# Three feature-major projections with token parts of 512, 512 and 32 moving columns in place of three of 352

## The reference, cut to what matters

```python
z = jnp.einsum('btd,de->bte', x, w_in)
mq, mk, mv, mo, mi, mf, aq, ak, av, iq, ik, iw = jnp.split(z, split_points, axis=-1)
mlstm = (heads(mq, M_HEADS), heads(mk, M_HEADS) * (M_HEAD_DIM ** -0.5), heads(mv, M_HEADS), mo, i_pre, log_f)
...
return h * jax.nn.sigmoid(o_pre), (C, n, m)      # o_pre is mo
```

## Time and profile before

| what | value |
|---|---|
| median of 3 runs | 1842.4 us (1838.47 to 1846.92) |
| the profiled execution's own time | 1841.46 us |
| its span, first to last instruction | 1839.6 us |
| mean granted TensorE clock | 0.954 of 2.4 GHz |
| PE busy | 1645.7 us (89% of the span) |
| DVE, ACT, POOL busy | 785.2, 471.7, 330.3 us |
| `fm` matmuls (L2090) | 864, in a stretch of 138.5 us |

### The profile page before, as it was taken

One profiled execution on the slowest core, in us unless ns is written; L12 is line 12 of the kernel. 1 busy time (PEld: TensorE's weight loads), 2 busy tenths in 40 slices (PEclk: granted clock), 3 DMA queues, 4 the chain that ended last, 5 costly groups with the idle time before them and its releaser, 6 DMA issues.

```text
span 1839.6 us, 28171 instructions
## 1 busy us (share of the span) xinstructions
PE 1645.7 (89%) x11020; PEld 1530.4 (83%) x11020; DVE 785.2 (43%) x1758; ACT 471.7 (26%) x942; POOL 330.3 (18%) x326
## 2 busy tenths in 40 slices
PE   7989999999987685887886899999999999999984
PEld 6855999999975564567886899999999999999983
DVE  2055999991224452254225532322322323313337
ACT  3264222121323342224114411111111111110013
POOL 3520452122200000100000322222221211212004
PEclk9979999999999898998997899999999999999996
DMA  5200211222243004113110321111111111111002
GB/s 161 70 7 26 65 51 48 90 89 94 71 126 130 13 24 162 46 46 128 44 45 1 92 69 47 47 42 31 51 41 47 46 47 47 46 46 46 1 23 95
DMA packets 122796, 110.36 MB, mean 60 GB/s; under 512 B 15778, under 2 KB 109606, under 8 KB 122674
## 3 DMA queue, kind: packets, MB, share of 16 engines
q1 hardware_dynamic: 122674, 108.61, 19.2%
HBM read 88.61 MB, written 19.95 MB: 59 GB/s over the span
## 4 chain that ended last, share of the span: by engine, by line
PE 41%; issue 14%; DVE 3%; ACT 0%; POOL 0%; DVEq 0%; ACTq 0%; POOLq 0%
PE bank L1577 27%; PE bank L1552 13%; DVE y_tm L1787 1%; DVE stats L1762 1%; PE bank L1008 0%; DVE y_acc L1560 0%; DVE hidden L1648 0%; ACT silu L1618 0%; POOL gate_up_split L1681 0%; DVE y_tm L1790 0%; PE bank L1719 0%; DVE hidden_split L1650 0%; PE bank L987 0%; PE bank L934 0%; POOL mv_by_sample L1137 0%
## 5 line engine op out<-in xcount | busy, mean ns | idle before, releaser
L1577 PE MATMUL bank<-x_split,gate_up_split 128*128 128x352 f32 x3168 | 517.0, 324 | 13.3 <-POOL gate_up_split L1681 6.6
L1577 PEld LDWEIGHTS bank<-x_split,gate_up_split 128*128 128x128 f32 x3168 | 510.5, 189 | 15.3 <-POOL gate_up_split L1681 6.9
L1552 PE MATMUL bank<-hidden_split,weight_split 128*128 128x352 f32 x1584 | 263.8, 326 | 15.7 <-DVE y_acc L1560 13.6
L2031 PE MATMUL bank<-w_split,xT_split 128*128 128x256 f32 (+1 forms) x2160 | 268.3, 284 | 7.4 <-POOL w_split L2237 7.4
L1552 PEld LDWEIGHTS bank<-hidden_split,weight_split 128*128 128x128 f32 x1584 | 257.7, 190 | 19.7 <-DVE y_acc L1560 17.4
L2031 PEld LDWEIGHTS bank<-w_split,xT_split 128*128 128x128 f32 (+1 forms) x2160 | 258.2, 181 | 10.5 <-issue 8.2
L1648 DVE TENSOR_TENSOR hidden<-silu,bank 128x352 f32<-128x352 f32 x66 | 34.4, 521 | 414.2 <-ACT silu L1618 414.0
L1681 POOL TENSOR_TENSOR gate_up_split<-gate_up,gate_up_split 128x2048 fp32r<-128x2048 f32 x22 | 101.6, 4618 | 593.6 <-ACT gate_up_split L1610 593.6
L1560 DVE TENSOR_TENSOR y_acc<-y_acc,bank 128x352 f32<-128x352 f32 x264 | 136.3, 520 | 119.1 <-PE bank L1552 119.1
L2326 DVE TENSOR_SCALAR_CACHE_REDUCE chosen<-scores,level 128x384 uint8<-128x384 f32 (+2 forms) x198 | 174.3, 942 | 1.2
L2090 PE MATMUL bank<-xT_split,w_split 128*128 128x352 f32 x864 | 138.5, 323 | 0.0
(11 more groups left out here) (254 smaller groups left out, 1581.7 us busy)
## 6 DMA issues: line engine op xcount, KB each, us to landing
w_unit<-in_w_in_dram SPq DMA_DIRECT2D x16, 1024.0 KB, 5.6
gate_up<-in_w_gate_dram SPq DMA_DIRECT2D x22, 512.0 KB, 4.0
gate_up<-in_w_up_dram SPq DMA_DIRECT2D x22, 512.0 KB, 5.2
down_weight<-in_w_down_dram SPq DMA_DIRECT2D x11, 1024.0 KB, 5.0
scratch_dram<-feature_stage SPq DMA_DIRECT2D x36, 176.0 KB, 1.8
scores<-in_x_prompt_dram SPq DMA_DIRECT2D x8, 512.0 KB, 5.8
out_dram<-stage SPq DMA_DIRECT2D x32, 128.0 KB, 1.7
out_weight<-in_w_out_dram SPq DMA_DIRECT2D x8, 512.0 KB, 4.4
```

The source lines that it names most:

```text
L1552: mm = pe.matmul(PS[6 + n % 2][:, 0:CH], wds[:, a, k, d * P:(d + 1) * P], hs[:, 2 * s + k, b, c * CH:(c + 1) * CH], start=(k == 0 and (a, ...
L1577: mm = pe.matmul(PS[2 * c + w][:, 0:CH], gs[:, u, a, w, k, :], xs[:, b, k, c * CH:(c + 1) * CH], start=(k == 0 and (a, b) == PARTS[0]), st ...
L2031: mm = pe.matmul(bank[0:rows(i), 0:HALF], xs1[:, a, k, tile_cols(i)], w[:, b, k, :], start=(k == 0 and (a, b) == PARTS[0]), stop=(k == KD ...
```

## The change

The 1,056 tokens of the `fm` jobs are cut at 512 and 1024. Parts 0 and 1 have 512 tokens, all of them prompt tokens, and part 2 has the 32 sample tokens. The number of jobs, matmuls and weight loads stays. The staging ring has 4 slots of 512 columns, no longer 6 of 352, because it lies in a fixed place. The index projection's `ikf` job (L2039) keeps its parts of 352.

```diff
-STG, FST, HALF = 8, 6, 256
+STG, FST, HALF = 8, 4, 256
+FM_COLS = [slice(0, 512), slice(512, 1024), slice(1024, T)]
...
-        fstage = put("feature_stage", iqT_at + 2048, FST * CH).rearrange("p (s n) -> p s n", s=FST)
+        fstage = put("feature_stage", iqT_at + 2048, FST * 512).rearrange("p (s n) -> p s n", s=FST)
...
-                            sp.dma_start(fm_dram[("mk", "mq", "mo").index(g), m, :, c * CH:(c + 1) * CH],
-                                         fstage[:, f % FST, :]).then_inc(fstored[f % FST], 16)
+                            t = FM_COLS[c]
+                            sp.dma_start(fm_dram[("mk", "mq", "mo").index(g), m, :, t],
+                                         fstage[:, f % FST, 0:t.stop - t.start]).then_inc(fstored[f % FST], 16)
...
-                            mm = pe.matmul(bank[:, 0:CH], wsplit[n_unit % 2][:, a, k, (m % 2) * P:(m % 2 + 1) * P],
-                                           xs1[:, b, k, c * CH:(c + 1) * CH],
+                            mm = pe.matmul(bank[:, 0:FM_COLS[c].stop - FM_COLS[c].start],
+                                           wsplit[n_unit % 2][:, a, k, (m % 2) * P:(m % 2 + 1) * P],
+                                           xs1[:, b, k, FM_COLS[c]],
...
-                    out = act.activation(fstage[:, f % FST, :], bank[:, 0:CH],
+                    w = FM_COLS[c].stop - FM_COLS[c].start
+                    out = act.activation(fstage[:, f % FST, 0:w], bank[:, 0:w],
```

## The result

The changed kernel takes 1870.6 us, the median of 4 runs (1868.8 to 1876.5), against 1843.7 us before: a ratio of 1.0154 with a 95% interval of 1.0121 to 1.0188. It is slower by 26.9 us between the medians, or 28 us by the ratio, which is taken from the means; 1868 us was forecast, with 1858 to 1882 as the range. (The kernel before has one more run here than ahead of the prediction, which moves its median from 1842.4 to 1843.7 us.) The profiled execution took 1870.41 us, its span is 1868.6 us, 29.0 us longer than before.

The account below looks back on a forecast made before the run. The prediction took PE's pace to bound the `fm` stage, with nothing behind it that has slack. 1841.5 us + 26.6 for 288 triples - 0.6 at the seam gave 1867.5, stated as 1868 us, range 1858 to 1882.

Parts of the forecast that it names:

- The place: The `fm` stage (L2090): PE's pace is its one bound, and each microsecond it ends later starts attention one later.
- The narrow matmul: 32-column matmuls of the `fm` jobs: the weight load sets the pace, 113 ns each, bounds 35 and 188 ns.
- The wide matmul: 512-column matmuls of the `fm` jobs: 229.7 ns each by the line through 256 and 352 columns; bounds 226.7 and 232.8.
- The clock: PE's granted clock in the `fm` stage: the forecast had it held at 1.00, which is 2.4 GHz.
- Rival 3: Narrow `fm` jobs: the clock falls after all twelve, 1.7 us each, 20.4 us more, 1889 us; chance 10%.
- The sum: Whole kernel: 1841.5 us, + 26.6 for the `fm` triples, - 0.6 at the stage's end, 1867.5; stated as 1868 us.
- every later stage as long as before: Stages behind the `fm` jobs: unchanged in length, named as a sign that the forecast is right.
- The seam: End of the `fm` stage, before attention: shorter last copy and smaller last store give back 0.6 us.
- The copies: ACT's bank copies in the `fm` stage: all but the last run under PE's next job.
- the slots: The four staging slots: stores land in time, 14.2 us against 16.4 us over four jobs, so costed at nothing.
- the weights: Weight loads and splits of an `fm` unit: under 15 us of a unit growing from 23 to 27.5, costing nothing.
- Rivals 1, 2 and 4: `fm` matmuls: wide nearly free (1828 us, 4%); narrow loads hidden (1846 us, 7%); load, matmul in strict turn (1890 us, 5%).

Follow-up runs that it names:

- e_pair: The changed kernel with the two narrow jobs of each weight unit one behind the other: 1888.1 us, ratio 1.0251 to the kernel before.
- e_mix: The changed kernel with two wide matmuls and the narrow one side by side for each slice and product: 1866.4 us, ratio 1.0124 to the kernel before.
- e_464: The changed kernel with parts of 464, 464 and 128 columns: 1853.9 us, ratio 1.0048 to the kernel before.
- e_16loads: The changed kernel with 16 loads and matmuls in a narrow job in place of 24, moving as many columns: 1854.6 us, ratio 1.0064 to the kernel before.
- e_w32: The changed kernel with narrow jobs loading 32 of 128 weight columns: 1847.0 us, ratio 1.0013 to the kernel before.
- e_allw32: The changed kernel with 32 of 128 weight columns loaded in all jobs, wide ones too: 1845.6 us, one run.

## Why the prediction was right, by its own steps

**The place** was right: the chain of waits and the windows of before put the whole change on PE's pace, and every microsecond of the stage reached attention (+31.1 us at the first score matmul, 565.67 against 534.60). Not every one reached the end: 29.0 us in these two traces, 26.9 between the medians.

**The narrow matmul** was the step that decided, and its row was the right one. L609, a different format in a different stage, gave 113 ns, from 111 to 115; a load started every 111.7 ns. The job's mean of 107.5 ns is lower only because its first load is hidden and the wide job behind pays the last. It is shown by three edits that the load sets it: a quarter of the weight columns, two thirds of the loads, and four times the moving columns.

**The wide matmul** was a little too small: 229.7 ns by the line through 256 and 352 columns, 234.4 measured. Of the seven nanoseconds of fixed part that the line left, most aren't there: from 256 to 512 columns the line has 0.454 ns a column and leaves 2. Time is close to proportional; the upper bound of 232.8 was the nearer one, and the measured pace lies above it.

**The clock** is where a rival came in part, and where the forecast itself, with the clock held at 1.00, was wrong. Two of the twelve narrow jobs had a fall behind them, at 1.5 us each (7.24 and 7.23 us in place of 5.72). Rival 3 had the size of a fall right (1.7 us) and, with 10% for itself, was drawn as all or nothing, though the range for 8 in 10 did reach to falls after some of the jobs. e_pair and e_mix show that the narrow stretches bring the falls.

**The sum** then is: 26.6 forecast, + 2.7 for the wide ones (576 x 4.7 ns), - 0.6 for the narrow ones (12 jobs of 2.58 us, and 0.09 us for the open load in the wide job behind each of eleven, in place of 288 x 113 ns), + 3.0 for two falls = 31.7, against 31.8 in the records. So the stage was forecast 5 us too short. That the total came within 3 us of 1868 is in part luck: the prediction had every later stage as long as before, and the stages behind gave back some 2 us in these two traces and some 5 between the medians. "Every later stage as long as before" didn't come true.

**The seam** gave 0.7 us in place of 0.6: from PE's last record to DVE's first mask there were 536.69 - 534.05 = 2.6 us, now 567.32 - 565.39 = 1.9 us. The copies hid, the slots cost nothing, the weights came in time: ACT waited 135.6 us for PE in the stage and none for a store.

**Rivals 1, 2 and 4** are out: 512 columns cost 234.4 ns, not 160; a load doesn't run ahead of more than one matmul (e_mix); and load and matmul don't take turns (128 columns cost 109.6 ns, not 166). The Trainium skill (TensorE: Matmul & The Clock Gate, section Back-to-back issue gap) gives 131 ns for 512 columns in a stream of load and matmul pairs; the trace doesn't agree: 234.4 ns for these float32r matmuls.

## What to carry to other kernels

Price a float32r matmul at the larger of its moving columns (0.46 ns each here) and its weight load (112 ns for 128 columns here), and with a fixed number of matmuls don't cut off a remainder that is shorter than the load: three parts of 352, or 400, 400 and 256, cost the same within 1.3 us, while 512, 512 and 32 leave 288 loads with nothing to hide under. When a size isn't in the trace, look for the row that has the same weights and the same columns, in whatever stage or format, and read its pace from first to last start. A run of short matmuls can also cost the clock of the dense work behind it; set singly among wide ones they didn't (e_mix), but the load stayed exposed.

## What the runs showed of the hardware that wasn't expected

PE was never idle in the `fm` stage of e_pair, by its records, and yet the clock fell to 1.2 GHz in each stretch of two narrow jobs (5.2 us at full clock); after single ones of 2.6 us it fell twice in twelve. With 128 moving columns in narrow jobs just as long (e_464), with narrow jobs of 1.7 us (e_16loads) or 0.75 us (e_w32) it didn't fall in the stage; none in twelve, in one trace each, is too little against two in twelve to call that a difference. The weight load follows the granted clock: one every 111.7 ns at 2.4 GHz, every 213 ns at 1.2. And a matmul of float32r costs 0.455 to 0.462 ns a column from 256 to 512 columns at a granted 2.4 GHz, some 10% over one column a cycle, with 3 ns of its 234 put down to the load that runs under it (e_allw32).
